# Lag blocks laid out by transfers through device memory, and the context's work moved between the latents' scan steps

## The chip, the cores and the metric

The kernel runs on one core of a Trainium2 chip. The time is that of one launch, in device microseconds. The kernel before took 1921.28 us (median of three runs, 1921.07 to 1925.02). The names of the engines are: PE for the matrix engine, DVE for the vector engine, ACT for the scalar engine, POOL for GpSimd, and SP for the engine that here only issues transfers (SPq is its queue).

## The reference, cut to what matters

One layer of a hybrid model is applied to 128 context tokens and to 512 latent tokens (width 1024). Everything is float32.

```
h   = rmsnorm(x) * (1 + sc1) + sh1            # sc, sh, g: from silu(cond) @ w_mod, 6 parts of 1024
z   = h @ w_in  ->  u (512), cb, cc, ch (512 each)
y1  = gelu(ssm(u) + d_skip * u);  y1 = y1 * sigmoid(y1 @ w_glu + b_glu)      # two complex scans
y2  = cb * conv3(cc * ch)                     # width 3, along the tokens
x   = x + g1 * (concat(rmsnorm(y1), rmsnorm_heads(y2)) @ w_out)
h   = rmsnorm(x) * (1 + sc2) + sh2
x   = x + g2 * peer(h)    # per head: scores, top 16 of 16 x 16 key pairs, gather 16 rows of expert_u and expert_v
y   = rmsnorm(x)
```

The scan starts from zero for the context and from given states for the latents. The last states of the context's scan are outputs too.

## The kernel before, in words

The kernel is written out by hand: each engine has one list of instructions in a fixed order, and semaphores join the lists. Nothing is planned by a scheduler, so the order of the code is the order on the engine, and an instruction that waits holds back everything behind it on its engine.

The scans are done in chunks of Q = 8 tokens: 16 chunks for the context, 64 for the latents. On PE, `chunk_sums` (sixteen groups g, of which the last eight belong to the backward scan) forms what each chunk adds to the state; ACT copies each group from PSUM into `HH` (semaphore `s_ev`). Inside a chunk the output comes from lag blocks: 64 matmuls on PE (`k_mm`) give one block for each lag and channel group, DVE adds them up in `Ksb` (`lag_blocks`, semaphore `k_ev`), and they must then be spread out so that the eight positions of a chunk stand in eight partition groups. That spread matrix is `M` (128 partitions, 32 groups, 128 columns, 2 MB). In the kernel before, PE spreads it by 2 x 32 matmuls with a selecting matrix (`esel`, line 662, `m_mm`), and ACT copies eight PSUM banks into `M` (line 1217, `m_ev`).

DVE then runs the scan over the chunks: sixteen steps for the context (lines 1571 to 1575, `scan_ctx` after the last), then fifteen steps that advance the four segments of the latents' scan at once, on tiles four times as wide, and then for each of the segments 2, 3 and 4 a correction (`segment_products`, `segment_add`, `segment_store`, lines 1598 to 1609). `scan_lat` says that `HH` is complete. ACT turns one half of it round into `Hb` (line 1244, `hb_ready`).

The context's own chain goes: context outputs of the scan (PE lines 697 to 702), gelu, turning, the gate's matmul (line 749), and beside it twelve convolution tiles (`conv_ctx`, line 675, each counts one on `zc_mm`; `zc_mm` 4, 8 and 12 end the three groups of four), the convolution itself on DVE, two norms (`head_sums`, `spread_heads`, `token_sums`, `spread_root`), and the output projection (`out_ctx`, line 788, `zoc_mm`). After it come the residual, the second norm (lines 1656 to 1668), the first query and scores (PE lines 826 and 833), the first top-k on DVE (lines 1679 to 1731), and with the indices the first gather on POOL (line 1935).

The latents' scan outputs are `y_lat`, eight pieces of 64 matmul records each (lines 766 to 771). They need `hb_ready`. In the kernel before two of the eight are put ahead of the first query, and six behind the scores. `spread_experts` (line 864), which hands the first indices to DVE and so to POOL, stands behind all of them.

All loads go through the one queue of SP, in the order of its list: the modulation weights (`load_mod`, 1 MB each, n = 0 to 23), the convolution tiles (`load_conv_ctx`, 0.5 MB each, six buffers), the gate's and the output's weights. A load waits on SP for its buffer: `load_mod(n)` until slab n-2 has been used on PE, the tiles 6 and up until four tiles earlier have been used, `woA` for slab 23 (`mod_mm` 24).

## Time and profile before

| | |
|---|---|
| Median of three runs | 1921.28 us |
| The profiled execution, its own time | 1922.27 us |
| Its span | 1920.1 us |
| PE busy | 62% |
| DVE busy | 72% |
| ACT, POOL busy | 19%, 38% |
| DMA's rate, mean | 392 GB/s |
| Chain that ended last | DMA 43%, PE 28%, DVE 23% |

The span is that of the instructions; about 2 us of the execution lie outside of it. The shares are means over stages of different kinds: the change touches only the stage from about 110 us to the first gather at 215.6 us. Rows are read as: start in us, duration in us, engine, line, operation, tiles; an "x" and a number at the end counts the records that were merged (a float32 matmul leaves two), and a bracket tells how long the engine was idle before and what ended that.

### The profile page before, as it was taken

To read this page: it belongs to the slowest core of one execution; us is meant where nothing else is said; L and a number is where in the kernel's file an instruction comes from. 1 tells how busy PE (TensorE), PEld (TensorE's weight loads), DVE (VectorE), ACT (ScalarE), POOL (GpSimd) and SP (SyncE) were. 2 spreads that over 40 slices of the span, in tenths; PEclk is the share of its full clock that TensorE was granted. 3 is DMA by queue.
4 is the path that set the end of the run, shared out by engine and by line. 5 is a ranking of instruction groups with operands and counts; after the bars stand their busy time and mean duration, and the time that the engine had idled before them with its cause. 6 is when DMAs were issued, how large, how long until landed. Compare 5 with 4: busy or idle time off the path is not lost.

```text
span 1920.1 us, 21154 instructions
## 1 busy us (share of the span) xinstructions
PE 1194.3 (62%) x7716; PEld 475.8 (25%) x7716; DVE 1382.6 (72%) x3664; ACT 373.5 (19%) x845; POOL 725.1 (38%) x666
## 2 busy tenths in 40 slices
PE   6989898999777777775543343544343454444434
PEld 3569644444322322221110000111000011111001
DVE  8968567777766766669777776677777678766664
ACT  5142441121122121111211110121111121111110
POOL 0000233344444434445434444444444354444440
PEclk9999999999878877775755555565555565555555
DMA  9855699999999999999999999999999999999994
GB/s 372 328 209 199 257 395 414 378 416 420 390 421 399 419 422 421 420 389 422 420 422 423 421 421 421 421 421 421 422 422 421 421 421 418 422 420 421 418 420 182
DMA packets 120968, 753.16 MB, mean 392 GB/s; under 512 B 12240, under 2 KB 27856, under 8 KB 33568
## 3 DMA queue, kind: packets, MB, share of 16 engines
q0 software_dynamic: 92160, 671.13, 84.5%
q1 hardware_dynamic: 28704, 80.69, 11.0%
q8 instruction: 60, 0.98, 0.2%
q14 instruction: 44, 0.36, 0.0%
HBM read 749.12 MB, written 11.04 MB: 396 GB/s over the span
## 4 chain that ended last, share of the span: by engine, by line
DMA 43%; PE 28%; DVE 23%; issue 2%; POOL 1%; ACT 1%; SPq 0%; DVEq 0%; POOLq 0%; ACTq 0%
DMA r<-table,gidx 31%; DVE r L1747 9%; DMA mix_r<-table,gidx 8%; PE bank L878 7%; PE bank L846 6%; PE bank L983 3%; DMA r<-w_mod 3%; DVE mix_r L1747 2%; PE bank L996 2%; PE bank L813 1%; POOL r L1935 1%; PE bank L962 1%; PE bank L855 1%; DVE i L1680 1%; PE bank L788 1%
## 5 line engine op out<-in xcount | busy, mean ns | idle before, releaser
L1935 POOL DMA_INDIRECT r<-table,gidx x542 | 607.7, 1121 | 865.3 <-PE bank L878 723.9
L1747 DVE CUSTOM_DVE_ANT_0 r<-r 128x1024 f32<-128x1024 f32 x542 | 658.1, 1220 | 246.5 <-DMA r<-table,gidx 246.0
L878 PE MATMUL bank<-r,cond 128*32 128x512 f32 x1432 | 327.2, 911 | 370.4 <-DVE cond L1759 295.2
L878 PE MATMUL bank<-r,wgt 128*32 128x512 f32 x736 | 166.8, 921 | 194.1 <-DVE wgt L1759 145.8
L1289 ACT ACTIVATE r<-r 128x2 f32<-128x2 f32 x320 | 65.1, 204 | 1013.1 <-DVE r L1747 1012.5
L878 PEld LDWEIGHTS bank<-r,cond 128*32 128x32 f32 x1432 | 37.1, 129 | 572.0 <-DVE cond L1759 437.2
L1935 POOL DMA_INDIRECT mix_r<-table,gidx x98 | 109.4, 1116 | 136.1 <-PE bank L878 117.0
L1747 DVE CUSTOM_DVE_ANT_0 mix_r<-mix_r,r 128x1024 f32<-128x1024 f32 x98 | 119.3, 1221 | 48.4 <-DMA mix_r<-table,gidx 48.2
L878 PE MATMUL bank<-mix_r,cond 128*32 128x512 f32 x264 | 91.1, 994 | 80.7 <-DVE cond L1759 63.4
L846 PE MATMUL bank<-hT_r,r 128*128 128x512 f32 x256 | 121.5, 630 | 0.9 <-ACT hT_r L1143 0.9
L878 PEld LDWEIGHTS bank<-r,wgt 128*32 128x32 f32 x736 | 18.9, 130 | 295.3 <-DVE wgt L1759 214.3
L1757 DVE SCALAR_TENSOR_TENSOR cond<-fold,r 128x32 f32<-128x32 f32 x168 | 34.8, 248 | 71.5 <-ACT r L1289 71.5
L846 PEld LDWEIGHTS bank<-hT_r,r 128*128 128x128 f32 x256 | 50.6, 203 | 75.8 <-issue 75.8
L1289 ACT ACT_TABLE_LOAD x51 | 65.4, 1283 | 0.9
L878 PE MATMUL bank<-mix_r,wgt 128*32 128x512 f32 x128 | 40.2, 930 | 38.2 <-DVE wgt L1759 35.6
L996 PE MATMUL bank<-mix_r,r 128*128 128x512 f32 x128 | 60.0, 611 | 0.0
L983 PE MATMUL bank<-hT_r,r 128*128 128x512 f32 x128 | 59.1, 604 | 0.0
L864 PEld LDWEIGHTS bank<-r,ident 128*32 128x32 f32 x1280 | 44.4, 140 | 43.6 <-DVE r L1719 36.8
L1747 DVE DVE_READ_ACCUMULATOR2_ANT r<- 128x1 f32 x640 | 52.6, 82 | 0.0
L1285 ACT ACT_TABLE_LOAD x40 | 51.3, 1283 | 0.7
L903 PE MATMUL bank<-mix_r,modrow 128*128 128x512 f32 x80 | 46.1, 712 | 3.2 <-ACT r L1304 1.9
L1757 DVE SCALAR_TENSOR_TENSOR wgt<-fold,r 128x32 f32<-128x32 f32 x88 | 18.3, 249 | 41.3 <-ACT r L1289 41.3
(367 smaller groups left out, 1637.1 us busy)
## 6 DMA issues: line engine op xcount, KB each, us to landing
r<-w_mod SPq DMA_DIRECT2D x24, 1024.0 KB, 9.7
r<-wq_heads SPq DMA_DIRECT2D x14, 1024.0 KB, 8.8
r<-table,gidx POOLq DMA_INDIRECT x542, 18.7
wq_heads<-w_query SPq DMA_DIRECT2D x8, 1024.0 KB, 12.1
r<-w_tiles SPq DMA_DIRECT2D x12, 512.0 KB, 7.8
x_r<-w_tiles SPq DMA_DIRECT2D x10, 512.0 KB, 6.0
hT_r<-xT SPq DMA_DIRECT2D x4, 640.0 KB, 6.1
r<-w_u SPq DMA_DIRECT2D x1, 2048.0 KB, 29.5
```

The costliest lines, as they stand in the source:

```text
L788: last = mm(bank[3 + m // 4][:, (m % 4) * P:(m % 4 + 1) * P], w[:, k, :], mixc[:, k, :], start=first and m in (0, 6) and k == ks[0], stop= ...
L846: last = mm(bank[2 + h][:, :], wqb[:, k, h * P:(h + 1) * P], hT[:, k, CTX:T], start=(k == 0), stop=(k == KD - 1))
L864: last = mm(bank[3][TG * s:TG * s + TG, 8 * tg:8 * tg + 8], ident[:, TG * tg:TG * tg + TG], gi[:, :, 4 * s:4 * s + 4], start=True, stop=True)
L878: last = mm(bank[ACC[b % 2][h]][to:to + TG, :], pair_weights(NPR * G + g)[:, e, :], rows[SLOT[G * TOPK + k]][:, D + h * 512:D + (h + 1) * ...
L903: last = mm(bank[at[h]][:, :], modrow[:, tg // 2, tg % 2 * P:(tg % 2 + 1) * P], h2tok[:, 512 * h:512 * h + 512], start=True, stop=True)
L983: last = mm(bank[(4, 5, 7)[r]][:, :], wtl[(tile + 2) % 3][:, k, :], hT[:, k, CTX:T], start=(k == 0), stop=(k == KD - 1))
L996: last = mm(bank[OUT_BANK[m % 3]][:, :], woA[:, m % 4, k, :], mixl[:, k, :], start=(k == 0), stop=(k == KD - 1))
L1285: A(e16, top, ACT.Exp, bias=small[:, 0:1], accum_out=small[:, 1:2]).then_inc(exp_done, 1)
L1289: A(gel[:, par, 2 * g:2 * g + 2], hid[:, par, 2 * g:2 * g + 2], ACT.Gelu_apprx_tanh).then_inc(gelu_done, 1)
L1747: V.tensor_tensor_reduce(row, row, h2r[tg], 1.0, 0.0, ALU.mult, ALU.add, hid[:, par, k:k + 1]).then_inc(dot_done, 1)
L1757: last = stt(pair_weights(n)[:, e, :], fold[:, :], gel[:, par, k:k + 1], gate[:, par, k:k + 1].broadcast_to([P, TG]), ALU.mult, ALU.mult)
L1935: G_.indirect_dma_start(rows[SLOT[j]], None, table, bass.IndirectOffsetOnAxis(gidx[:, e, k:k + 1], 0)).then_inc(row_in[SLOT[j]], 16)
```

## The change

The selecting matmuls and ACT's eight copies go. Instead SP writes `Ksb` to a tensor in device memory (`kfull`, 480 KB), waits for that, and reads it back by eight transfers into `M`. Each of them reads 512-byte pieces, 16 x 32 of them, and writes 16 partitions (256 KB). The context's outputs wait for these (`m_in`).

On PE the lag blocks' matmuls come ahead of groups 8 to 15 of the chunk sums; the first eight convolution tiles come ahead of the context's outputs, with the modulation slabs 20 and 21 between; slabs 22 and 23 come behind the outputs; the heads' norm comes ahead of the output projection, whose convolution half now is first; and all eight pieces of `y_lat` stand behind the first scores. On DVE `lag_blocks` comes first, four of the sixteen groups are copied by DVE in place of ACT (`s_back`), the two half-width products of a scan step become one of full width, the context's elementwise work is put between the fifteen latent steps, and the residual and the second norm come ahead of the segments 3 and 4. On SP the loads of the slabs 20 to 23 come behind the new transfers and behind the tiles 6 and 7.

```diff
@@ SP
-            for n in range(18, 24):
-                load_mod(n)
+            load_mod(18)
+            load_mod(19)
+            sp.wait_ge(k_ev, 1)
+            sp.dma_start(kfull.rearrange("(m p) x -> p m x", p=P), Ksb).then_inc(k_out, 16)
+            sp.wait_ge(s_mm, 8)
+            sp.wait_ge(k_out, 16)
+            lags = kfull.rearrange("(g i) x -> i g x", i=GC)
+            for i in range(Q):
+                sp.dma_start(M[GC * i:GC * i + GC, :, :], lags[:, :, (Q - 1 - i) * GC:(Q - 1 - i) * GC + P]).then_inc(m_in, 16)
             sp.wait_ge(zc_mm, 2)
             ...
             for q in range(6, 8):
                 load_conv_ctx(q)
-            sp.wait_ge(m_mm, 2)
+            for n in range(20, 24):
+                load_mod(n)
@@ PE
-            pe.wait_ge(k_ev, 1)
-            pe.wait_ge(s_ev, 16)
-            for a in range(2):
-                for s in range(Q):
             ...
-                mod_slab(20 + a)
-            mod_slab(22)
             ...
+            conv_ctx(0)
+            conv_ctx(1)
+            mod_slab(20)
+            mod_slab(21)
+            pe.wait_ge(m_in, 16 * Q)
+            pe.wait_ge(s_ev, 12)
+            pe.wait_ge(s_back, 4)
             ...
-            mod_slab(23)
-            conv_ctx(1)
+            conv_ctx(2)
             ...
             pe.wait_ge(ld_wo, 32)
-            out_ctx(True, range(KS), 1)
-            out_ctx(False, range(KS, KD), 2)
+            out_ctx(True, range(KS, KD), 1)
+            out_ctx(False, range(KS), 2)
             ...
-            y_lat(0, 2)
-            y_lat(0, 3)
-            for i in range(4):
-                y_lat(1, i)
+            pe.wait_ge(hb_ready, 1)
+            pe.wait_ge(mod_free, 6)
+            for n in range(2):
+                for i in range(4):
+                    y_lat(n, i)
@@ DVE
-                link(tt(ta, prev, re, ALU.mult),
-                     tt(tb[:, :, 0, :], prev[:, :, 1, :], im[:, :, 0, :], ALU.mult),
-                     tt(tb[:, :, 1, :], prev[:, :, 0, :], im[:, :, 1, :], ALU.mult))
+                link(tt(ta, prev, re, ALU.mult), tt(tb, prev[:, :, ::-1, :], im, ALU.mult))
             ...
+            advance_rest(1, 7)
             ...
+            advance_rest(7, 10)
+            dve.wait_ge(zc_mm, 12)
             ...
+            advance_rest(10, 12)
```

The order on SP's queue before, from the modulation slabs on. `w_mod` are the slabs (x6 counts 18 to 23), `w_tiles` with a wait on `zc_mm` are first the gate's two tiles, then the convolution tiles:

```order
L411 DMA r<-w_mod 128x2048 [waits mod_mm] x6
L447 DMA r<-w_tiles 128x1024 [waits zc_mm]
L447 DMA r<-w_tiles 128x1024
L416 DMA x_r<-w_tiles 128x1024 [waits zc_mm] x2
L451 DMA mix_r<-w_query 128x8x256 [waits m_mm]
```

And in the changed kernel:

```order
L412 DMA r<-w_mod 128x2048 [waits mod_mm] x2
L447 DMA kfull<-mix_r 128x4x240 [waits k_ev]
L452 DMA r<-kfull 16x32x128 [waits k_out,s_mm]
L452 DMA r<-kfull 16x32x128 x7
L455 DMA r<-w_tiles 128x1024 [waits zc_mm]
L455 DMA r<-w_tiles 128x1024
L417 DMA x_r<-w_tiles 128x1024 [waits zc_mm] x2
L412 DMA r<-w_mod 128x2048 [waits mod_mm] x4
L460 DMA mix_r<-w_query 128x8x256
```

The write and the eight reads now stand ahead of the gate's tiles, of the tiles 6 and 7, and of four of the six slabs.

On PE, the changed kernel between the sixth convolution tile and the gelu of the context's outputs (L673 is a convolution tile, L537 a modulation slab, L695 to L700 the outputs, L709 their turning):

```order
L673 MATMUL bank<-hT_r,x_r 128x128 [waits wtc_in0]
...
L673 MATMUL bank<-hT_r,x_r 128x128 [waits wtc_in1]
...
L537 MATMUL bank<-r,cond 32x256 [waits wm_in0]
...
L537 MATMUL bank<-r,cond 32x256 [waits wm_in1]
...
L695 MATMUL bank<-r 32x128 [waits k_ev,s_back,hbc_ready,s_ev,m_in]
...
L697 MATMUL bank<-r 16x128 x8
...
L537 MATMUL bank<-r,cond 32x256 [waits wm_in0]
...
L709 MATMUL bank<-ident,r 128x128 [waits yc_gelu]
```

Before, the same outputs came ahead of every convolution tile:

```order
L662 MATMUL bank<-mix_r,wgt 32x512 [waits s_ev,k_ev]
...
L528 MATMUL bank<-r,cond 32x256 [waits wm_in0]
...
L662 MATMUL bank<-mix_r,wgt 32x512 [waits m_ev] x2
...
L697 MATMUL bank<-r 32x128 [waits hbc_ready,m_ev]
...
L675 MATMUL bank<-hT_r,r 128x128 [waits wtc_in4,m_ev]
```

So the tiles' and the slabs' loads are now waited for ahead of the outputs.

On DVE, the changed kernel from the residual's second half to the first top-k (L1598 to L1609 are a segment's correction, L1663 and L1670 to L1674 the second norm, L1679 raises `scan_lat`, L1689 is the top-k):

```order
L1656 SCALAR_TENSOR_TENSOR x_r<-bank,modT,x_r 128x128 [waits zoc_mm]
...
L1599 TENSOR_TENSOR r<-r 128x1024
L1663 RECIPROCAL frs<-frs 128x1 [waits rms_c,dve_seq]
...
L1603 TENSOR_TENSOR r<-r 128x1024
...
L1670 TENSOR_TENSOR hT_r<-x_r,bank 128x4x128 [waits x1c_ready,inv_mm,dve_seq]
...
L1674 TENSOR_SCALAR hT_r<-hT_r,gs,modT 128x128 [waits mod_ready,dve_seq]
...
L1598 TENSOR_TENSOR r<-r 128x1024
...
L1679 COPY small<-eps_c 128x1 [waits dve_seq]
...
L1689 MAX r<-r 128x8 [waits sc_ev]
```

Before, all segments and `scan_lat` (L1650) came ahead of the residual:

```order
L1603 TENSOR_TENSOR r<-r 128x1024 [waits dve_seq]
...
L1650 COPY small<-eps_c 128x1 [waits dve_seq]
L1656 SCALAR_TENSOR_TENSOR x_r<-bank,modT,x_r 128x128 [waits zoc_mm,ld_xc]
...
L1659 RECIPROCAL frs<-frs 128x1 [waits rms_c]
...
L1664 TENSOR_TENSOR hT_r<-x_r,bank 128x4x128 [waits x1c_ready,inv_mm]
...
L1679 MAX r<-r 128x8 [waits sc_ev]
```

Two of the three later segments are behind the residual now, and with them `scan_lat`.

## Rows read from the trace of the kernel before

**Rows 1.** Windows: busy PE, PEld, DVE, ACT, POOL; granted clock, DMA share, GB/s

```profile
215.00:505.00 290.00, 269.75 (x1381) 130.19 (x1381) 198.79 (x541) 75.39 (x142) 109.34 (x98) 0.98 0.99 403
...
900.00:1400.00 500.00, 229.17 (x1304) 54.61 (x1304) 370.19 (x969) 78.64 (x183) 217.59 (x199) 0.55 1.01 421
```

**Rows 2.** Timeline, all engines, from the end of the segments to the first gather

```profile
188.14 0.15 DVE L1650 COPY small<-eps_c 128x1 f32<-128x1 f32 x1
188.33 1.91 ACT L1244 ACTIVATE r<-r 128x2048 f32<-128x2048 f32 x1 [9.03 <-DVE small L1650]
...
203.72 0.66 PE L766 MATMUL bank<-r 128*64 128x128 f32 x8
204.31 0.49 DVE L1679 MAX8 r<-r 128x8 f32<-128x128 f32 x2 [4.48 <-ACT r L1270]
...
213.99 0.88 PE L864 MATMUL bank<-r,ident 128*32 128x8 f32 x32
...
215.11 0.17 DVE L1731 CAST gidx<-bank 128x16 uint32<-128x16 f32 x1
...
215.58 1.12 POOL L1935 DMA_INDIRECT r<-table,gidx  x1 [48.58 <-DVE gidx L1731]
```

**Rows 3.** Timeline of PE and DVE: lag blocks, context's outputs, first convolution tiles

```profile
109.66 1.07 PE L528 MATMUL bank<-r,cond 128*32 128x256 f32 x16
...
116.66 1.82 PE L645 MATMUL bank<-r 128*32 128x128 f32 x57
120.09 2.06 PE L645 MATMUL bank<-r 128*32 128x128 f32 x68 [1.60 <-issue]
...
122.38 0.69 DVE L1557 COPY mix_r<-bank 128x512 f32<-128x512 f32 x1 [1.43 <-PE bank L645]
...
137.58 0.65 PE L697 MATMUL bank<-r 128*32 128x128 f32 x16 [1.57 <-ACT r L1219]
...
144.87 3.84 PE L675 MATMUL bank<-hT_r,r 128*128 128x128 f32 x32
```

**Rows 4.** Timeline of DVE: first products of successive scan steps, context, then latents

```profile
118.04 0.22 DVE L1571 TENSOR_TENSOR mix_r<-r,AR 128x64 f32<-128x64 f32 x1
...
119.02 0.23 DVE L1571 TENSOR_TENSOR mix_r<-r,AR 128x64 f32<-128x64 f32 x1
...
136.69 0.42 DVE L1571 TENSOR_TENSOR r<-r,AR 128x256 f32<-128x256 f32 x1
...
138.47 0.43 DVE L1571 TENSOR_TENSOR r<-r,AR 128x256 f32<-128x256 f32 x1
```

**Rows 5.** Issues of transfers: count, KB of each, median us to landing

```profile
x_r<-xT SPq DMA_DIRECT2D x1, 512.0 KB, 4.4
```

**Rows 6.** The two gate tiles (0.5 MB each) on an idle queue, line 447

```profile
L447 SPq DMA_DIRECT2D r<-w_tiles x2: 328/380/433, 148.7 to 149.1; - x2
...
DMA to landing us min/median/max: 3.7/4.2/4.6
```

**Rows 7.** Timeline of PE and DVE from the convolution to the second norm

```profile
164.13 1.11 DVE L1619 TENSOR_SCALAR mix_r<-mix_r,colv 128x128 f32<-128x128 f32 x4
...
173.11 1.95 PE L675 MATMUL bank<-hT_r,x_r 128*128 128x128 f32 x16
...
183.09 1.22 DVE L1598 TENSOR_TENSOR r<-r 128x1024 f32<-128x1024 f32 x1
185.51 3.74 PE L788 MATMUL bank<-mix_r,r 128*128 128x128 f32 x32
...
192.86 1.13 DVE L1656 SCALAR_TENSOR_TENSOR x_r<-bank,modT,x_r 128x128 f32<-128x128 f32 x4 [2.38 <-PE bank L788]
...
197.37 0.69 DVE L1664 TENSOR_TENSOR hT_r<-x_r,bank 128x512 f32<-128x512 f32 x1 [0.51 <-PE bank L731]
```

**Rows 8.** Timeline of PE: the same sixteen matmuls after a wait, and next

```profile
537.49 8.91 PE L846 MATMUL bank<-hT_r,r 128*128 128x512 f32 x16 [0.94 <-ACT hT_r L1143]
...
547.32 7.13 PE L846 MATMUL bank<-hT_r,r 128*128 128x512 f32 x16
```

More of the change, by code:

```diff
@@ L621, in _, with chunk_sums @@
             mod_slab(16)
-            pe.wait_ge(bpt_ev, 17)
-            for g in range(16):
-                if g >= 2:
-                    pe.wait_ge(s_ev, g - 1)
+            def chunk_sums(g):
+                if g >= 10 and g % 2:
+                    pe.wait_ge(s_back, (g - 9) // 2)
+                elif g >= 2:
+                    pe.wait_ge(s_ev, min(g - 1, 4 + g // 2))
                 for j in range(2):
@@ L633, in _ @@
                 last.then_inc(s_mm, 1)
-                if g == 7:
-                    mod_slab(17)
+            pe.wait_ge(bpt_ev, 17)
+            for g in range(8):
+                chunk_sums(g)
+            mod_slab(17)
             pe.wait_ge(bd_ready, 1)
@@ L647, in _ @@
                 last.then_inc(k_mm, 1)
+            for g in range(8, 16):
+                chunk_sums(g)
             mod_slab(18)
             mod_slab(19)
[L652 to L666 removed]
             def conv_ctx(r):
[L670 removed]
                 for i in range(4):
@@ L751, in _ @@
             mod_turn(2)
-            conv_ctx(2)
+            head_sums()
+            spread_heads()
             def y_lat(n, i, terms=range(5)):
@@ L779, in out_ctx @@
                 for m in (0, 1, 2, 3, 6, 7, 4, 5) if first else range(KD):
-                    if first and m == 2:
-                        head_sums()
                     if first and m == 6:
-                        spread_heads()
+                        pe.wait_ge(sqc_ready, 2)
+                        token_sums(256, sqx[0], True, True)
+                    if first and m == 4:
+                        spread_root(0)
                     if m == 4:
@@ L1201, in _ @@
             act.wait_ge(bp_ready, 2)
-            for g in range(16):
+            for g in (*range(8), *range(8, 16, 2)):
                 d, pr = g // 8, (g % 8) * 2
@@ L1212, in _ @@
                 last.then_inc(s_ev, 1)
-            for n in range(8):
-                a, j = n // 4, n % 4
-                act.wait_ge(m_mm, a + 1)
-                A(M[:, 2 * j + a::8, :], bank[MBANK[a][j]][:, :].rearrange("p (q x) -> p q x", q=4), ACT.Copy).then_inc(m_ev, 1)
+            act.wait_ge(zc_mm, 4)
+            A(ccx.rearrange("p k t -> p (k t)"), bank[0][:, :], ACT.Copy).then_inc(ccx_ev, 1)
             act.wait_ge(scan_ctx, 1)
@@ L1373, in _ @@
             take_scores(0)
+            act.wait_ge(scan_lat, 1)
+            A(Hb, HH[:, NCH - 1:NCC - 1:-1, :, 1, :], ACT.Copy).then_inc(hb_ready, 1)
             exps(0)
@@ L1578, in spread @@
                 return v[:, :, :].rearrange("p (a r) x -> p a r x", a=1).broadcast_to([P, n, 2, NQ])
-            dve.wait_ge(s_ev, 16)
+            lag_blocks()
+            for g in range(9, 16, 2):
+                pr = g % 8 * 2
+                dve.wait_ge(s_mm, g + 1)
+                for r in range(2):
+                    src = bank[4 + g % 2][:, 0:4 * NCH].rearrange("p (q r c) -> p c r q", q=2, r=2)[:, :, r, :]
+                    V.tensor_copy(HH[:, NCC:0:-1, r, 1, pr:pr + 2], src[:, 0:NCC, :])
+                    last = V.tensor_copy(HH[:, NCH - 1:NCC:-1, r, 1, pr:pr + 2], src[:, NCC + 1:NCH, :])
+                last.then_inc(s_back, 1)
+            dve.wait_ge(s_back, 4)
+            dve.wait_ge(s_ev, 12)
             link(V.tensor_copy(fin[:, :, :], HHs[:, NCC, :, :]))
@@ L1590, in _, with advance_rest @@
             rest = slice(1, NJ)
-            for i in range(1, SEG):
-                link(advance(seg[:, rest, i - 1, :, :], seg[:, rest, i, :, :], many_a, many_b, spread(AR, NJ - 1), spread(AI, NJ - 1)))
+            def advance_rest(lo, hi):
+                for i in range(lo, hi):
+                    link(advance(seg[:, rest, i - 1, :, :], seg[:, rest, i, :, :], many_a, many_b, spread(AR, NJ - 1), spread(AI, NJ - 1)))
             def segment_products(j):
@@ L1669, in _ @@
             last.then_inc(xsc_ready, 1)
+            segment_products(4)
+            segment_add(4)
+            segment_store(4)
+            V.tensor_copy(small[:, 2:3], eps_c[:, :]).then_inc(scan_lat, 1)
             NT = 23
```

105 lines of the change are left out of this document (40 added, 65 removed).

## Prediction

> **What bounds the kernel now.** I read the windows first, to see which stage the change can touch. After the first gather the DMA engines are busy all the time, at 403 GB/s to 505 us and at 421 GB/s from 900 to 1400 us [rows 1]: the gathers are one stream that runs at the rate of the memory until the end. Whatever comes before the first gather is a lead-in. If the first gather starts later by some us, the end does too, since nothing behind it has slack to give back. So the whole question is when the cast of the first indices (line 1731) ends: at 215.11 + 0.17 = 215.3 us in the kernel before, and POOL follows 0.3 us later [rows 2].
>
> Next the timeline around it. DVE ends its top-k before PE lets it go on: PE starts `spread_experts` (line 864) at 213.99, right behind the last of six `y_lat` pieces, which began at 203.72 [rows 2]. That is 10.27 / 6 = 1.71 us a piece. So the first gather hangs on the end of `y_lat`, and DVE's own work only through the start of the top-k at 204.31.
>
> **The rule for break-even.** In the changed kernel all eight pieces stand behind the scores and wait for `Hb`. They take 8 x 1.71 = 13.7 us, and `Hb` takes 0.2 + 1.9 us after `scan_lat` (188.14 to 190.24) [rows 2]. To be as early as before, `y_lat` must start at 214.0 - 13.7 = 200.3, so `scan_lat` must be there at about 198.2 us. It was at 188.1 before, with nothing but DVE's own work ahead of it. The change puts in front of it the residual, the second norm and the wait for the output projection.
>
> **Part 1, up to the end of the context's scan.** The lag matmuls took from 116.66 to 122.2, with a gap of 1.6 us in them [rows 3]. Moved ahead of eight chunk sums, they start when slab 17 ends, at 109.66 + 1.07 = 110.7 [rows 3], and end at 116.3. `lag_blocks` takes 1.7 us on DVE, which is idle then: `k_ev` at 118.0. The eight chunk sums follow in the 6.0 us that they took before (110.7 to 116.66): 122.3. Four copies on DVE instead of ACT hide beside them, the last adds 0.6, the start of the scan 0.5: 123.4 instead of 118.04. A context step takes 119.02 - 118.04 = 0.98 us [rows 4]. Two products of 32 columns become one of 64. I take 0.92, because the second start (0.10 us) goes and the longer product costs about 0.04; the bounds are 0.88 and 1.0. Sixteen steps are 14.7: `scan_ctx` at 138.1 instead of 136.7, although 3.1 us of `lag_blocks` and its wait have left the scan. A latent step takes 1.78 [rows 4] and by the same reckoning 1.72 after, so 0.9 us over fifteen.
>
> **Part 2, the transfers.** This is where the price is. A 0.5 MB load on an idle queue lands after 3.7 us, and the one behind it 1.3 us later [rows 6] (148.7 + 3.7 and 149.1 + 4.6). So a load costs 1.3 us of the queue per 0.5 MB and 2.4 us once (1.4 ahead, 1.0 behind). 1 MB costs 2.6. The write of `kfull` (480 KB) then costs about 1.6 + 2.4: issued at 118.0, in at 122.0. The reads may only then be issued, and their data start at 123.4.
>
> How long is a read of 256 KB into 16 partitions? The trace has none. The lower bound: a 0.5 MB load in pieces of 512 bytes over 128 partitions took 4.4 us [rows 5], so 2.0 on the queue, and half the bytes take 1.0 us. The upper bound: 1 MB over 128 partitions puts 8 KB in each in 2.6 us; if what a partition takes in is the limit, 16 KB a partition need 5.2 us. I take the middle by ratio, 2.3 us each and 18.4 for the eight, since the narrow target must cost something and neither row is near to it. All end at 141.8.
>
> The Trainium skill, page "SBUF — State Buffer", section "Door 1: The DMA port swizzle", says that DMA bandwidth depends on how many of sixteen ports the partitions reach, and gives 104 GB/s for the partitions 0 to 15, against 328 for all. An estimate from that is 2.5 us a transfer, and the end would be 1.6 us later than by my 2.3. The same page, section "Can I just issue two DMAs to hit both halves?", says that two such transfers to different partitions serialize, so the eight would not overlap either. No row here shows a narrow transfer.
>
> Behind them on the queue stand: the gate's two tiles (2.6), tile 6 (1.3, lands at 146.7), tile 7 (148.0), slab 20 (150.6), slab 21 (153.2). PE meanwhile: slabs 18 and 19 to 124.3, six convolution tiles of 1.84 each (a quarter of the 7.3 us that four take: 3.84 and its like [rows 3]) to 135.3. Then it waits 11 us for tile 6. Two tiles and the slab 20 are done by about 153, and slab 21 waits for its load: 154.2. A cost that this hides: after a wait of this kind PE's clock is at 1.2 instead of 2.4 GHz for a while. Sixteen matmul records that began after PE had been waiting took 8.91 us, the same sixteen next 7.13 [rows 8], and the granted clock is a mean of 0.98 to 505 us and 0.55 from 900 us, where PE waits for most of the time [rows 1]. So 1.8 us more for the tiles 6 and 7, which fits in ahead of slab 21.
>
> The context's outputs take 137.58 to 144.87 = 7.3 us [rows 3]: 161.5. Slabs 22 and 23: 163.5. Only then SP issues `woA` (2 MB, 5.2 at the same rate), which stands ahead of the tiles 10 and 11: 163.5 + 1.4 + 5.2 + 1.3 + 1.0 gives tile 10 at 172.4, and two tiles end `zc_mm` 12 at about 176.0. Before it was at 173.11 + 1.95 = 175.06 [rows 7]. DVE has done six latent steps, the convolution and three more steps by 161.5 and waits 14 us. (The convolution is three groups of four instructions of 128 columns, 1.1 each [rows 7], and one product: 4.2.)
>
> **Part 3, from `zc_mm` 12 to the first gather.** PE: gate 3.7 (sixteen matmuls, as the 3.74 at 185.51 [rows 7]), `mod_turn` 1.2, `head_sums` 0.9: 181.8. Root and reciprocal 0.5, `spread_heads` 1.0, and the scaling by DVE (1.1), with one latent step and the hand-overs between: 185.0. Output projection: convolution half 7.4 (two of the 3.74 [rows 7]) and 1.1 for sums and root, then the other half 7.4: 201.0. This second half was in the kernel before the work of 185.5 to 192.7, so PE is 8.3 us later here. Residual 1.1, then DVE puts segment 3 (products 2.4, the rest 2.6) ahead of the norm's scaling: 207.3 against 197.37 [rows 7]. Scaling 2.4 and segment 4, as 183.09 to 188.14 = 5.0 [rows 2, 7]: `scan_lat` at 214.8. `Hb` 2.1, `y_lat` 13.7, `spread_experts` 0.9, cast 0.3: 231.8.
>
> **Sum.** 231.8 - 215.3 = 16.5 us later. The profiled execution took 1922.27 us, 1.0 above the median of the runs, so 1938.8 for it and 1937.8 by the median. What is removed (the selecting matmuls on PE and ACT's eight copies) is in these times already: PE has no shortage of time in part 2, it waits.
>
> **Rivals.**
> 1. The narrow transfers run like wide ones, 1.0 us each. Then all in part 2 moves up by 10.4 us: `zc_mm` 12 at 165.6, indices at 221.4, so 6.1 later: 1927.4. Even with free reads PE's own work sets part 2 and the indices come at about 219.4: 1925.4. For it: packets of 512 bytes cost little more than large ones. Against it: the target has an eighth of the partitions. At 5.2 us each it is 23 us worse than my sum, 1961.
> 2. Faster: DVE without waits. Work from 123.4 to the end of segment 4 is 14.7 + 25.8 (latent steps) + 4.2 (convolution) + 15.0 (segments) + 8.6 (residual, norms, products) = 68.3, so `scan_lat` at 191.7 and the indices at 208.7, 6.6 us earlier: 1914.7. It decides from the 6.4 us of waiting that DVE can afford before 198.2. For it: DVE waits for most of the time from 188.3 to 204.3 [rows 2], and the new order puts segments there. Against it: in part 3 alone DVE waits some 7 us, for head sums, roots and the projection, and 14 at tile 11.
> 3. The delay is absorbed: 1919 to 1924. The stage to 505 us has PE busy 93% [rows 1], not DMA alone, so a shifted start could meet fewer collisions. Against it: that work too is queued behind the first indices.
>
> **Numbers.** Forecast (late by narrow transfers, 1933 to 1944) 0.58; rival 1 at 1.0 to 1.4 us a transfer 0.22; the dear end, over 1944, 0.06; absorbed 0.08; faster 0.06. Small and large misses in the chain are some us each way. The range that leaves out no more than 2 in 10 is 1925 to 1944. A measurement tells apart 0.2%, 3.8 us, so slower is over 1925.1: 0.58 + 0.06 + most of 0.22, 0.84; same 0.10; faster 0.06.
>
> **What would show it.** The rows of the eight reads: median to landing, and when the last is in (141.8 + 1.0 by me, 132 by rival 1). PE's wait ahead of the seventh convolution tile, for a load, about 11 us. DVE's wait for the twelfth tile, 14 us. `y_lat` in one piece of 13.7 us, ahead of line 864's successor, starting at 216.9. If `scan_lat` comes before 198 us, the forecast is wrong at its root; if the cast is at 231.8 and the end is not 16 us later, the stream of gathers was not the bound that I read.

## The result and the profile after

The changed kernel takes 1955.03 us (median of 6 runs, 1952.33 to 1956.74), the kernel before 1923.45 in the same runs (1921.07 to 1927.53). The ratio is 1.0158 with a 95% interval of 1.0148 to 1.0168, so the change costs 30.4 us, 28.5 to 32.3. Forecast were 16.5 us, and the range ended at 1944. The profiled span is 1954.9 us against 1920.1.

The timeline after, PE, DVE and POOL (start us, duration, engine, line, operation; in brackets the idle time before it and what ended it):

```profile
147.33 6.57 PE L673 MATMUL bank<-hT_r,x_r 128*128 128x128 f32 x32 [11.94 <-DMA x_r<-w_tiles]
...
153.83 1.93 PE L537 MATMUL bank<-r,cond 128*32 128x256 f32 x32
155.58 0.62 PE L695 MATMUL bank<-r 128*32 128x128 f32 x16
...
160.60 0.42 PE L695 MATMUL bank<-r 128*32 128x128 f32 x8
164.62 0.66 PE L695 MATMUL bank<-r 128*32 128x128 f32 x8 [3.59 <-issue]
...
180.07 5.47 PE L673 MATMUL bank<-hT_r,x_r 128*128 128x128 f32 x32 [4.97 <-DMA x_r<-w_tiles]
...
185.64 0.69 DVE L1623 TENSOR_TENSOR mix_r<-mix_r,bank 128x512 f32<-128x512 f32 x1 [22.28 <-PE bank L673]
...
194.69 6.76 PE L788 MATMUL bank<-mix_r,r 128*128 128x128 f32 x32 [1.61 <-DVE mix_r L1631]
...
220.91 5.65 PE L821 MATMUL bank<-hT_r,mix_r 128*128 128x128 f32 x32 [3.45 <-ACT hT_r L1139]
...
230.01 0.66 PE L765 MATMUL bank<-r 128*64 128x128 f32 x8 [2.27 <-ACT r L1365]
...
245.13 0.88 PE L859 MATMUL bank<-r,ident 128*32 128x8 f32 x32
...
246.72 1.13 POOL L1945 DMA_INDIRECT r<-table,gidx  x1 [55.69 <-DVE gidx L1741]
```

The large waits lie where the forecast put them. PE stands 11.9 us for the seventh convolution tile (line 673), and 5.0 us for tile 10; the outputs (line 695) start at 155.6; DVE waits 22.3 us for the last tile (line 1623). All eight pieces of `y_lat` run as one block from 230.01 to 245.13, and the first gather comes at 246.72 instead of 215.58 [rows 2]: 31.1 us later, and the span is 34.8 us longer. The block of work is the same; it is later, and slower. Two tiles that took 3.84 us [rows 3] take 6.57 here, the first projection group 6.76 instead of 3.74 [rows 7], and inside the outputs PE waits 3.59 us for nothing that the profile shows.

The page's issues and the windows of the transfers (windows: length; busy us of PE, PEld, DVE, ACT, POOL; granted clock; DMA share; GB/s):

```profile
r<-kfull SPq DMA_DIRECT2D x8, 256.0 KB, 12.6
...
kfull<-mix_r SPq DMA_DIRECT2D x1, 480.0 KB, 4.1
```

```profile
122.00:128.00 6.00, 6.00 (x80) 4.98 (x79) 4.79 (x26) 0.29 (x3) 0.00 (x0) 1.00 1.19 121
128.00:134.00 6.00, 6.00 (x57) 6.00 (x55) 5.31 (x27) 0.60 (x1) 0.00 (x0) 1.00 1.29 106
134.00:140.00 6.00, 1.39 (x13) 1.20 (x11) 5.45 (x24) 1.47 (x2) 0.00 (x0) 0.95 1.24 107
140.00:146.00 6.00, 0.00 (x0) 0.00 (x0) 5.66 (x15) 0.44 (x1) 0.00 (x0) 0.50 1.08 290
```

From 128 to 140 us, with the reads at the head of the queue, the DMA engines move 106 and 107 GB/s. 256 KB at that rate are 2.5 us a read, where I had taken 2.3, and in the trace the eight reads land from 126.12 to 143.65 us, 2.50 us apart in the mean. The Trainium skill's page "SBUF — State Buffer", section "Door 1: The DMA port swizzle", gives 104 GB/s, measured at 1 MiB, for partitions 0 to 15. This trace agrees, and for eight groups of 16 partitions.

One window answers where the 31 us went: from 110 us to the start of the first `spread_experts` (line 864 before, 859 after), before and after:

```profile
110.00:213.99 103.99, 97.83 (x1597) 82.81 (x1589) 77.13 (x258) 30.28 (x79) 0.61 (x1) 1.00 0.51 185
```

```profile
110.00:245.13 135.13, 101.17 (x1457) 89.89 (x1445) 76.87 (x240) 24.41 (x54) 0.61 (x1) 0.85 0.56 159
```

PE was idle for 104.0 - 97.8 = 6.2 us and is now idle for 135.1 - 101.2 = 34.0, so 27.8 more. It is busy 3.3 us longer although the 64 selecting matmuls (8.7 us; an f32 matmul is two records in the trace, so 128 of them) are gone: the rest of the work takes 12.1 us more at a mean clock of 0.85. 27.8 + 12.1 - 8.7 is 31.1, up to rounding. DVE's work adds nothing to it; DVE is busy for 77 us in both.

### The profile page after: what moved, and what is told of

Its sections match the earlier page's. It is cut to its first block, busy times and chain, and to the rows that moved or that the text cites. A ratio compares the mean times of both kernels' runs of the same rounds, so it can differ in the third digit from the quotient of the medians.

```text
span 1954.9 us, 20863 instructions
## 1 busy us (share of the span) xinstructions
PE 1202.6 (62%) x7588; PEld 483.3 (25%) x7588; DVE 1383.0 (71%) x3646; ACT 368.0 (19%) x822; POOL 729.7 (37%) x666
## 3 DMA queue, kind: packets, MB, share of 16 engines
q1 hardware_dynamic: 33456, 83.28, 12.1%
## 4 chain that ended last, share of the span: by engine, by line
DMA 38%; PE 32%; DVE 24%; issue 3%; ACT 2%; POOL 1%; DVEq 0%; SPq 0%; POOLq 0%; ACTq 0%
DMA r<-table,gidx 28%; DVE r L1757 9%; DMA mix_r<-table,gidx 8%; PE bank L873 7%; PE bank L841 6%; PE bank L978 3%; PE bank L991 2%; DVE mix_r L1757 2%; PE bank L808 1%; POOL r L1945 1%; PE bank L585 1%; DMA x_r<-w_tiles 1%; PE bank L673 1%; PE bank L537 1%; PE bank L898 1%
## 5 line engine op out<-in xcount | busy, mean ns | idle before, releaser
L873 PE MATMUL bank<-mix_r,wgt 128*32 128x512 f32 x128 | 40.3, 945 | 35.0 <-DVE wgt L1769 32.3
L898 PE MATMUL bank<-mix_r,modrow 128*128 128x512 f32 x80 | 50.3, 769 | 3.2 <-ACT r L1294 1.9
L859 PE MATMUL bank<-r,ident 128*32 128x8 f32 x1280 | 47.1, 196 | 1.4 <-DVE r L1729 1.4
## 6 DMA issues: line engine op xcount, KB each, us to landing
wq_heads<-w_query SPq DMA_DIRECT2D x8, 1024.0 KB, 11.1
```

The source lines that it names most:

```text
L859: last = mm(bank[3][TG * s:TG * s + TG, 8 * tg:8 * tg + 8], ident[:, TG * tg:TG * tg + TG], gi[:, :, 4 * s:4 * s + 4], start=True, stop=True)
L873: last = mm(bank[ACC[b % 2][h]][to:to + TG, :], pair_weights(NPR * G + g)[:, e, :], rows[SLOT[G * TOPK + k]][:, D + h * 512:D + (h + 1) * ...
L898: last = mm(bank[at[h]][:, :], modrow[:, tg // 2, tg % 2 * P:(tg % 2 + 1) * P], h2tok[:, 512 * h:512 * h + 512], start=True, stop=True)
```

## The experiments

Ratios are against the kernel before, run on the same chip each time. The first gather's start is from the profiled execution; it was 215.58 before and 246.72 after.

| run | us | ratio (95%) | first gather |
|---|---|---|---|
| e1 after, M spread on PE | 1949.3 | 1.0139 (1.0122 to 1.0156) | 240.01 |
| e2 after, wide reads | 1946.0 | 1.0118 (1.0101 to 1.0136) | 237.60 |
| e3 after, half the bytes | 1944.3 | 1.0113 (1.0096 to 1.0131) | 235.28 |
| e4 before, with the transfers | 1945.6 | 1.0116 (1.0099 to 1.0134) | 237.03 |
| e5 e1, tiles ahead of woA | 1941.7 | 1.0098 (1.0073 to 1.0123) | 236.22 |
| e6 after, tiles ahead of woA | 1945.7 | 1.0121 (1.0098 to 1.0144) | 241.67 |
| e7 e1, tail of before | 1952.2 | 1.0156 (1.0134 to 1.0178) | 243.60 |
| e8 e5, tail of before | 1945.5 | 1.0121 (1.0098 to 1.0145) | 239.33 |
| e9 after, PE kept busy (too long) | 1968.0 | 1.0230 (1.0212 to 1.0248) | 259.05 |
| e10 e5, no loads beside outputs | 1947.8 | 1.0123 (1.0106 to 1.0140) | 238.35 |
| e11 e6, transfers on ACT's queue | 1950.3 | 1.0136 (1.0119 to 1.0153) | 242.85 |
| e12 before, merged products | 1921.2 | 0.9986 (0.9977 to 0.9996) | 213.34 |
| e13 after, PE kept busy | 1947.4 | 1.0128 (1.0109 to 1.0146) | 239.11 |
| e14 e5, last tiles ahead of outputs | 1939.3 | 1.0089 (1.0069 to 1.0108) | 227.64 |
| e15 e14, first query's load later | 1940.2 | 1.0085 (1.0063 to 1.0108) | 231.78 |

**e1: the order without the transfers.**

```diff
@@ SP
-            sp.dma_start(kfull.rearrange("(m p) x -> p m x", p=P), Ksb).then_inc(k_out, 16)
             ...
@@ PE
+            spread_lags(0)          # the selecting matmuls, 32 each
             ...
             conv_ctx(0)
             ...
+            spread_lags(1)
             conv_ctx(1)
-            pe.wait_ge(m_in, 16 * Q)
+            pe.wait_ge(m_ev, 8)     # ACT's eight copies into M
```

> The changed kernel, but the lag blocks are spread as in the kernel before: 64 selecting matmuls in two lots (ahead of the convolution's tiles 0 to 3 and of 4 to 7) and eight copies on ACT; no transfer through device memory. Everything else keeps the new order. Theory A (the eight narrow reads hold everything behind them on SP's queue, and the order itself is harmless): tile 6 is there when PE wants it, DVE's wait of 22.3 us ahead of the context's last convolution product falls under 4 us, the first gather comes at 216 to 222 us instead of 246.7, and the time is 1920 to 1930 us. Theory B (the new order costs by itself: latents' outputs in one piece behind the last scan step, convolution and norms ahead of the scan): the first gather stays later than 228 us and the time over 1933 us.

Tile 6 was on time, but theory A fell: 27 of the 30 us stay, and the gather and the time are where theory B had them. Which part of the order costs, this run does not tell; e5 to e8 ask that. DVE waited nearly as long as in the changed kernel (timeline of PE and DVE):

```profile
171.97 6.22 PE L666 MATMUL bank<-hT_r,x_r 128*128 128x128 f32 x32 [5.92 <-DMA x_r<-w_tiles]
...
178.31 0.69 DVE L1639 TENSOR_TENSOR mix_r<-mix_r,bank 128x512 f32<-128x512 f32 x1 [20.39 <-PE bank L666]
```

**e2, e3: the price of a read.**

```diff
# e2
-                sp.dma_start(M[GC * i:GC * i + GC, :, :], lags[:, :, (Q - 1 - i) * GC:(Q - 1 - i) * GC + P]).then_inc(m_in, 16)
+                sp.dma_start(M[:, 4 * i:4 * i + 4, :], lags[:, :, (Q - 1 - i) * GC:(Q - 1 - i) * GC + P]).then_inc(m_in, 16)
# e3
-                sp.dma_start(M[GC * i:GC * i + GC, :, :], lags[:, :, ...])
+                sp.dma_start(M[GC * i:GC * i + GC, 0:16, :], lags[:, 0:16, ...])
```

> The changed kernel with eight reads of the same 256 KB in pieces of the same 512 bytes, but each into all 128 partitions instead of 16 (M then holds the lag blocks in the wrong places; this part of the computation is left wrong). Theory A (the price is that of 16 partitions): the reads take 0.7 to 1.0 us each instead of 2.3 to 2.6, the last lands by 131 us instead of 144, tile 6 starts before 138 us instead of 147.3, and the time is 1918 to 1930 us. Rival (the price is that of 512-byte pieces, or of a read behind a write): nothing moves, 1952 to 1957 us.

> The changed kernel with eight reads of half the bytes each (128 KB, groups 0 to 15; groups 16 to 31 of M are left as they were, so that part of the computation is left out). Theory A (a read costs by its bytes into 16 partitions): each takes 1.2 us instead of 2.4, tile 6 starts near 138 us instead of 147.3, and the time falls by 8 to 14 us, to 1941 to 1947. Rival (a price per transfer, whatever its bytes): tile 6 moves by less than 3 us, time 1950 to 1956 us.

Windows of e2, then the row of tile 6 in the timeline of PE, of e2 and of e3:

```profile
122.00:128.00 6.00, 6.00 (x80) 4.98 (x79) 4.82 (x26) 0.27 (x3) 0.00 (x0) 1.00 1.04 271
128.00:134.00 6.00, 6.00 (x57) 6.00 (x56) 5.31 (x27) 0.60 (x1) 0.00 (x0) 1.00 1.03 303
```

```profile
136.21 3.84 PE L673 MATMUL bank<-hT_r,x_r 128*128 128x128 f32 x32 [0.84 <-DMA x_r<-w_tiles]
```

```profile
136.37 3.84 PE L673 MATMUL bank<-hT_r,x_r 128*128 128x128 f32 x32 [1.49 <-DMA x_r<-w_tiles]
```

The same bytes in the same pieces move at 271 to 303 GB/s into 128 partitions (the second window holds other loads too), so 0.9 us a read. Tile 6 came 11.1 us earlier with wide reads, and 11.0 with half the bytes, so the reads do cost what I said, and e3 falls into theory A's range. But e2 misses it by 16 us: the times fell by only 7.7 us (1.0158 to 1.0118) and 8.7, the first gather by 9.1 and 11.4. The other 22 to 23 us have another cause.

**e4: the transfers in the old order.**

```diff
@@ SP
             load_mod(19)
+            sp.dma_start(kfull.rearrange("(m p) x -> p m x", p=P), Ksb).then_inc(k_out, 16)
             ...
@@ PE
-            for a in range(2):      # the selecting matmuls
             ...
+            pe.wait_ge(m_in, 16 * Q)
```

> The kernel before with the transfers alone: the lag blocks go through device memory with the same write and eight reads, while DVE, the convolution, norms and the latents' outputs keep the old order (lag blocks inside the context's scan, k_ev at about 122 us; the context's outputs ahead of the convolution). Theory A: the write starts at about 125 us and the reads end at about 150; the outputs start at 150 to 153 instead of 137.6 us, the convolution's tiles 0 to 5 lie behind them, and the time is 1933 to 1948 us. Theory B (the transfers are mostly hidden and the new order costs): 1920 to 1928 us.

Windows of e4, then its timeline of PE:

```profile
122.00:128.00 6.00, 0.33 (x7) 0.00 (x0) 5.38 (x32) 0.00 (x0) 0.00 (x0) 0.90 0.50 125
128.00:134.00 6.00, 0.00 (x0) 0.00 (x0) 5.38 (x31) 0.00 (x0) 0.00 (x0) 0.50 1.27 101
...
140.00:146.00 6.00, 0.00 (x0) 0.00 (x0) 5.66 (x17) 0.00 (x0) 0.00 (x0) 0.50 1.28 106
```

```profile
150.46 1.93 PE L536 MATMUL bank<-r,cond 128*32 128x256 f32 x16 [28.14 <-DMA r<-w_mod]
...
157.42 1.93 PE L536 MATMUL bank<-r,cond 128*32 128x256 f32 x16 [2.18 <-DMA r<-w_mod]
159.13 1.08 PE L694 MATMUL bank<-r 128*32 128x128 f32 x16
```

Here the queue alone does it: slab 20 stands behind the reads, PE is idle for 28.1 us, and the outputs start at 159.1 (forecast 150 to 153: the slabs 20 to 22, which stand behind the reads, I had left out; the time is in theory A's range). So either half of the change costs 22 to 27 us by itself, and both together 30. That the two do not add fits DVE's waits: it stands still for convolution tiles at much the same time in all three kernels, 20.4 us in e1 (to 178.3) and 22.3 with both (to 185.6), for the twelfth tile, and 22.0 in e4 (161.7 to 183.7), for the eighth. In the kernel before it has no such wait.

**e5 to e8: what the order's delay hangs on.** In e5 and e6 SP's order, in e7 and e8 DVE's and PE's tail:

```diff
# e5 on e1, e6 on after
-            for q in range(8, 10):
+            for q in range(8, 12):
                 load_conv_ctx(q)
             sp.wait_ge(mod_mm, 24)
             sp.dma_start(woA, w_o[:, 0:4, :, :]).then_inc(ld_wo, 16)
-            for q in range(10, 12):
-                load_conv_ctx(q)
# e7 on e1, e8 on e5: DVE, then PE
+            segment_products(3)
             ...
+            V.tensor_copy(small[:, 2:3], eps_c[:, :]).then_inc(scan_lat, 1)
             residual_ctx(0)
@@
+            y_lat(0, 0)
             ...
             spread_root(1)
+            y_lat(0, 1, range(1, 5))
```

> The kernel of the first experiment (new order, lag blocks spread by PE and ACT) with one more edit: SP issues the convolution's tiles 10 and 11 ahead of woA (2 MB) instead of behind it. In the first experiment PE waited 5.9 us for tile 10 and then ran two tiles at the low clock, so that DVE stood still for 20.4 us. Theory C (the new order makes DVE's whole queue wait for the last convolution tile, and each us of that wait comes out at the end one for one): the wait falls by 8 us, the time is 1938 to 1944 us against 1949. Theory D (the delay is that of the tail, latents' outputs in one piece behind a scan that ends behind the residual): less than 3 us, over 1946.

> The changed kernel with the tiles 10 and 11 issued ahead of woA, nothing else. Theory C: PE's wait of 5.0 us for tile 10 and the 1.7 us of low clock behind it go, the time falls by 5 to 8 us, to 1947 to 1950 us. Theory D: no more than 2 us, 1953 to 1957.

> The kernel of the first experiment with the tail of the kernel before: DVE does the latents' segments 3 and 4 ahead of the context's residual and norm, and PE does two of the eight pieces of the latents' outputs ahead of the first query. Theory C: DVE is 27 us late already by its waits, so this moves work about: the time falls by 1 to 5 us, to 1944 to 1948. Theory D (the tail is the cost): it falls by more than 15 us, to under 1934.

> The first experiment's kernel with both edits, the tiles 10 and 11 ahead of woA and the tail of the kernel before. Theory C: the two gains add, 1935 to 1942 us. Theory D: as the tail alone gives, under 1934. Either way it is the new order's head (convolution ahead of the outputs and norms among the scan's steps) that is left in it.

Tiles that no longer stand behind a 2 MB load gave 7.9 us (1.0139 to 1.0098) and 7.1 (1.0158 to 1.0121), as theory C said. In the profiled execution of e5 PE no longer waits for tile 10 (5.9 us in e1), but DVE's wait fell by 2.4 us only, to 18.0, and not by the 8 expected: it was the slowest of the four (1944.7 us), and the gaps in its outputs were 6.6 us against 3.0 in e1 (below). The old tail gave nothing: e7 and e8 are 3.3 and 4.4 us slower than e1 and e5, with intervals that overlap. Theory D is dead, and theory C, which had both faster, missed these two. With the segments and `scan_lat` ahead of the residual PE stood 9.8 us for the residual's squares (timeline of PE, e7):

```profile
216.55 1.86 PE L727 MATMUL bank<-ones,mix_r 128*128 128x1 f32 x8 [9.81 <-ACT mix_r L1267]
```

The two halves of the tail, DVE's and PE's, were not tried one by one.

**e9, e13: the clock.** Matmuls that nothing uses stand where PE would wait; e13 has half of them.

```diff
+            def keep_warm(b, n):
+                for _ in range(n):
+                    mm(bank[b][:, :], ident[:, :], hT[:, 0, CTX:T], start=True, stop=True)
@@ conv_ctx
+                    if q == 6:
                         ...
+                        keep_warm(3, 13)      # e9: 25
+                    if q == 10:
                         ...
+                        keep_warm(0, 5)       # e9: 10
@@ ahead of the projection, the query and y_lat
+            keep_warm(3, 1)                   # then 3 and 2; e9: 4, 7 and 4
```

> The changed kernel with matmuls added that compute nothing used, where PE stands still: 25 of 128x512 ahead of the convolution's tile 6 (11.1 us at full clock, in a wait of 11.9), 10 ahead of tile 10 (4.4 in 5.0), 4 ahead of the output projection, 7 ahead of the first query (3.1 in 3.5), 4 ahead of the latents' outputs. Theory E (PE's low clock after each wait costs 11 us of the 31: PE is busy for 101.2 us from 110 us to the first spread of the expert indices, where the same work without the spread took some 90 before): the granted clock is 0.97 or more in this stretch, the tiles 6 and 7 take 3.8 us instead of 6.6, the first half of the projection 3.9 instead of 6.8, the query 3.9 instead of 5.7, and the time falls by 5 to 10 us, to 1945 to 1950 us. Rival (the low clock lies beside other waits): less than 2 us, 1953 to 1957 us.

> The changed kernel with matmuls of 128x512 added that compute nothing used (0.87 us each, as e9 showed): 13 ahead of the convolution's tile 6 (11.3 us in a wait of 11.9), 5 ahead of tile 10 (4.3 in 5.0), 1 ahead of the output projection, 3 ahead of the first query (2.6 in 3.5), 2 ahead of the latents' outputs (1.7 in 2.3). Theory E (PE's low clock behind its waits is 11 us of its busy time, and more than half of that on the path): the time falls by 5 to 10 us against the changed kernel's 1955, to 1945 to 1950 us. Rival: the low clock lies beside other waits, less than 2 us, 1953 to 1957.

One such matmul takes 0.87 us, not the 0.44 I had planned with (I had read a record for a matmul), so in e9 they outlasted every wait and cost 14 us. In e13 they fit (timeline of PE, then a window as above):

```profile
149.34 3.84 PE L685 MATMUL bank<-hT_r,x_r 128*128 128x128 f32 x32 [2.47 <-DMA x_r<-w_tiles]
...
192.51 3.81 PE L800 MATMUL bank<-mix_r,r 128*128 128x128 f32 x32 [0.55 <-DVE mix_r L1646]
```

```profile
110.00:237.53 127.53, 112.79 (x1513) 89.25 (x1505) 76.83 (x240) 24.70 (x55) 0.61 (x1) 0.97 0.62 170
```

The clock is 0.97 instead of 0.85, and the 24 added matmuls are 23.3 of the 112.8 us busy (three of them ran partly at the low clock), so the kernel's own work takes 89.5 us instead of 101.2. In the kernel before it is 97.8 - 8.7 = 89.1, so nearly all that the work grew by is the clock's. The first gather is 7.6 us earlier (0.9 of them from a shorter gap in the outputs), the time 5.8 us less (1.0158 to 1.0128). Theory E holds, at the low side of its range. The Trainium skill, page "TensorE: Matmul & The Clock Gate", section "What's actually happening", puts the penalty of the ramp, the work done before the clock is up, at under 1% of a typical kernel's span. This case agrees: what e13 took off is 0.3% of the span, though it is a fifth of what the change costs.

**e10, e15: the gaps in the outputs.** The outputs are 160 small matmuls (320 records) in 7 us.

```diff
# e10 on e5
+            sp.wait_ge(yc_mm, 2)
             for n in range(22, 24):
                 load_mod(n)
# e15 on e14
+            sp.wait_ge(yc_mm, 2)
             sp.dma_start(wqa, w_query[:, :, 0:DQ]).then_inc(ld_first, 16)
```

> The kernel with the lag blocks spread by PE and the tiles 10 and 11 ahead of woA, with one wait more on SP: the slabs 22 and 23, and so all loads behind them, are issued only when the context's outputs are done, so that no load runs beside the outputs. Theory F (the gaps of 2.5 and 4.1 us in the 320 small matmuls of the outputs, in which PE waits for nothing that the profile shows, come from its instructions arriving late behind the loads; in the kernel before, with the DMA engines 5% busy there, the gap was 0.3 us): the gaps fall under 0.7 us in all and the outputs take 7.0 to 8.0 us instead of 13.6; PE then waits 3 to 6 us for slab 22, and the time is 1938 to 1944 us. Rival (the gaps belong to the place in the program, whatever the DMA engines do): they stay over 3 us, and the time is 1943 to 1950.

> As e14, but the first query's weights (1 MB) are loaded only behind the context's outputs, so that, where the slabs 22 and 23 have landed by then, nothing loads beside the outputs. Theory F (PE's gaps in the outputs come from its instructions arriving late behind loads): the gaps in the outputs fall under 1.5 us in all, and the time is 2 to 5 us under that of e14. Rival: no difference over 1 us.

The timeline of PE and the window of the outputs, of e5, then of e10:

```profile
154.06 0.32 PE L710 MATMUL bank<-r 64*16 64x128 f32 x5 [2.45 <-issue]
...
161.08 0.80 PE L705 MATMUL bank<-r 128*32 128x128 f32 x9 [4.13 <-issue]
```

```profile
148.78:163.68 14.90, 8.32 (x325) 5.70 (x317) 8.09 (x24) 0.00 (x0) 0.00 (x0) 0.86 0.96 350
```

```profile
155.32 0.49 PE L708 MATMUL bank<-r 128*32 128x128 f32 x9 [1.12 <-issue]
...
161.83 1.93 PE L531 MATMUL bank<-r,cond 128*32 128x256 f32 x16 [4.94 <-DMA r<-w_mod]
```

```profile
148.61:156.89 8.28, 7.16 (x324) 5.10 (x316) 7.90 (x24) 0.01 (x1) 0.00 (x0) 1.00 0.02 7
```

With the DMA engines 96% busy the gaps are 6.6 us and the outputs take 14.9; with 2% they are 1.1 us, and 8.3. So the loads beside them make the gaps, as theory F said, apart from a rest of 1.1 (I had said under 0.7). What PE waits for can be read from the traces too. They have packets of 16 KB and of the kind `instruction`, on a queue of their own (section 3 of the changed kernel's page: packets, MB, share of the 16 engines):

```profile
q8 instruction: 59, 0.97, 0.2%
```

From 100 to 260 us of the 17 traces there are 52 gaps of more than 0.3 us in which PE waits for no semaphore, and each ends 1.2 to 1.6 us after one of these packets has landed. In the 39 gaps of up to 2 us the packet had started 0.7 to 2.2 us before PE stopped; in the 13 longer ones it started only after PE had stopped. In e5 the gaps begin at 151.62 and 156.95, the packets run from 151.79 to 152.72 and from 158.78 to 159.76, and PE goes on at 154.06 and 161.08. In e10 the packet of the gap that is left started at 152.93, and PE stopped at 154.20. So it is code that PE waits for, and beside loads the code's packet starts late. That this queue is PE's own is inferred from these times. The kernel before fits: its 26% (the expectation has 5%) are loads that land by 139.9 us, and its gap of 0.3 comes at 142.6.

The gain is lost at once. PE then waits 4.9 us for slab 22, and e10 at 1.0123 is no faster than e5 at 1.0098; its time is in the rival's range. In e15 the gaps are 0.8 us against 2.0 in e14, and the time is the same (1.0085 and 1.0089): theory F is right about the gaps and the rival about the time.

**e11: another queue.**

```diff
-            sp.dma_start(kfull.rearrange("(m p) x -> p m x", p=P), Ksb).then_inc(k_out, 16)
+            act.dma_start(kfull.rearrange("(m p) x -> p m x", p=P), Ksb).then_inc(k_out, 16)
             ...     # and the eight reads
```

> The changed kernel with the tiles 10 and 11 ahead of woA, and the write and the eight reads of the lag blocks issued by ACT on its own queue instead of SP's. Theory A (tile 6 waits because it stands behind the reads on one queue): tile 6 starts at 135 to 140 us instead of 148.7, the reads end at 144 to 150, and the time falls by 3 to 9 us against the same kernel on SP's queue (1945.7), to 1937 to 1943. Rival (the reads fill the DMA engines that every load needs, whatever the queue): tile 6 starts after 145 us, 1944 to 1948.

The timeline of PE:

```profile
145.62 5.41 PE L665 MATMUL bank<-hT_r,x_r 128*128 128x128 f32 x32 [10.78 <-DMA x_r<-w_tiles]
...
155.70 1.91 PE L529 MATMUL bank<-r,cond 128*32 128x256 f32 x16 [3.67 <-DMA r<-w_mod]
158.77 1.08 PE L687 MATMUL bank<-r 128*32 128x128 f32 x16 [1.15 <-DMA r<-kfull]
```

SP issued tile 6 at 129.5 us, where it was 134.6 in e6, and still it landed only at 145.6, 3.1 us earlier than in e6, and PE waited 10.8 us for it. The rival holds for tile 6, and the time is even above its range (1.0136 against e6's 1.0121, with intervals that overlap): the narrow reads fill the engines that every load needs, and standing behind them on one queue is at most 3 us of the wait. The loads on the other queue did pass reads: the last three of the eight landed at 150.7, 156.8 and 158.7, behind tile 6, and the outputs waited for the last (158.77). The comparison is not quite clean, since ACT issued the write 3.2 us later than SP in e6, behind its own copies.

**e12: one part alone, on the kernel before.**

```diff
-                     tt(tb[:, :, 0, :], ...), tt(tb[:, :, 1, :], ...))
+                link(tt(ta, prev, re, ALU.mult), tt(tb, prev[:, :, ::-1, :], im, ALU.mult))
```

> The kernel before with one part of the change alone: on DVE the two products of a scan step that cross the real and imaginary halves are one instruction, 32 instructions less in the scan and three less in the segments. DVE's work to the last scan step is some 2.5 us shorter. Theory G (PE is the bound of this stretch: it is idle for 6.2 of 104 us): within 1.5 us of the kernel before. Rival (DVE's scan is the bound): 2 to 3 us faster.

The timeline of PE at the start of the outputs:

```profile
135.47 0.64 PE L697 MATMUL bank<-r 128*32 128x128 f32 x16 [0.90 <-ACT r L1219]
```

The time is in the rival's range: 2.7 us faster (0.8 to 4.4, which does not exclude theory G's 1.5). The outputs start at 135.47 instead of 137.58 [rows 3], behind the context's scan (0.8 of these 2.1 us is a shorter gap in the lag matmuls, which the edit does not touch). PE waits there in both kernels for ACT's copy of what the scan gives, 1.57 us before and 0.90 here. So up to there DVE is on the path of the kernel before, which I had read as PE's. This kernel is the only one that beats both.

**e14: DVE's wait taken away by order.**

```diff
             mod_slab(21)
+            pe.wait_ge(m_ev, 5)
+            conv_ctx(2)                 # loads: ahead of slabs 22 and 23
             ...                         # the context's outputs
+            head_sums()                 # ACT: its square ahead of the gelu
             mod_slab(22)
             ...
-            conv_ctx(2)
```

> The kernel e5 (lag blocks spread by PE and ACT, tiles 10 and 11 early) with the context's last four convolution tiles ahead of its outputs on PE (their loads ahead of the slabs 22 and 23), the head sums behind the outputs, and ACT's square for them ahead of the first gelu. Theory C (what is left in e5 is DVE standing still for 18 us for the last tile, since the scan's steps stand behind it): that wait falls under 3 us, a shorter one for the heads' root takes its place, the first gather comes at 222 to 230 us instead of 236.2, and the time is 1927 to 1936 us. Rival (the chain from the gate's product through the norms and the projection sets the end, and it hangs on the outputs): the gather moves by less than 3 us, 1939 to 1943.

The timeline of DVE and PE:

```profile
168.20 0.20 DVE L1643 RECIPROCAL frs<-frs 128x8 f32<-128x8 f32 x1 [6.82 <-ACT frs L1238]
...
202.30 5.15 PE L834 MATMUL bank<-hT_r,mix_r 128*128 128x128 f32 x32 [3.14 <-ACT hT_r L1152]
...
210.91 0.66 PE L778 MATMUL bank<-r 128*64 128x128 f32 x8 [2.27 <-ACT r L1382]
```

DVE's wait for the tile is gone, one of 6.8 us for the heads' root has come, and the gather is 8.6 us earlier, inside the range given. But the time is 3 us over its own range and inside the rival's, and 1.7 us under e5's by ratio, with intervals that overlap. The 8.6 us compare the slowest of e5's executions with the fastest of e14's four (1935.4). So the traces show that DVE's wait can be taken away by order; that this makes the kernel faster is not shown. What is left in e14 is a tail of short waits of PE (3.1, 2.3, 2.0, 1.1 us and less); other work was not tried in them.

## Why the prediction was wrong

Right were the bound (the first gather), the place and order of the large waits, and the price of a read: 2.5 us against 2.3. DVE's wait for the twelfth tile came where it was forecast, but took 22.3 us and not 14. Step by step, forecast against measured:

| | forecast | measured | difference |
|---|---|---|---|
| `scan_ctx` | 138.1 | 138.5 | 0.4 |
| tile 6 | 146.7 | 147.3 | 0.6 |
| outputs start | 154.2 | 155.6 | 1.4 |
| outputs end | 161.5 | 167.1 | 5.6 |
| `woA` issued | 163.5 | 170.6 | 7.1 |
| `zc_mm` 12 | 176.0 | 185.5 | 9.5 |
| `y_lat` starts | 216.9 | 230.0 | 13.1 |
| cast ends | 231.8 | 246.4 | 14.6 |

**The first failed step: "the context's outputs take 137.58 to 144.87 = 7.3 us".** I carried a duration over to a place with other traffic. They took 11.5 us, 4.2 more: 3.6 of gap, of the kind that e10 shows to come from the loads beside them, and the rest by the low clock behind the gap. The DMA engines were 26% busy in that stretch before, and 98% after (windows, before and after):

```profile
137.58:144.87 7.29, 6.99 (x320) 5.13 (x320) 6.88 (x21) 1.16 (x1) 0.00 (x0) 1.00 0.26 105
155.58:167.10 11.52, 7.93 (x328) 5.69 (x321) 7.41 (x22) 0.00 (x0) 0.00 (x0) 0.84 0.98 353
```

**The second: "So 1.8 us more for the tiles 6 and 7, which fits in ahead of slab 21."** I charged the clock once. In the trace it was at 0.50 six times between 139 and 235 us, each time behind waits or gaps, short ones too: it cost 2.7 us in the tiles 6 and 7, 1.5 in the slabs 22 and 23, 1.7 in the tiles 10 and 11, 3.0 in the projection, 1.8 in the query, 1.4 in `y_lat`. The last five are 9.4 us; with the 4.2 of the outputs and the 1.4 by which they started late that is 15.0, against the 14.6 of the table. In e13, where the clock stays up, the gather is 7.6 us earlier. The row that I quoted for it (8.91 against 7.13 us [rows 8]) was too mild: a group behind a wait took up to 1.8 times its length here (6.76 us for 3.74).

**The third is in a rival.** "Even with free reads ... the indices come at about 219.4: 1925.4." e1, with no reads, had its gather at 240.0, and e2, with reads at 0.9 us, 1946 us instead of 1927. There I was wrong by 19 us, more than in the forecast itself. I had worked out the order's own cost as a by-product of the reads' and never by itself: it has the same gap in the outputs, the same clock, and the same 2 MB load ahead of tile 10. By e1 and e4 each of the two costs 22 to 27 us alone, so a range that begins at 1925 left out what the order costs.

Rival 2 (faster) fell on DVE: from the start of the scan to the end of segment 4 it worked 64 us (reckoned: 68.3), but it also waited 39, 22 of them in one place. Rival 3 (absorbed) fell too: the span's delay is 1.0 to 1.2 times that of the first gather in most runs, 34.8 for 31.1 here. What the extra 1 to 5 us are was not looked into.

## What to carry to other kernels

When an engine has no idle time in a stretch, an order is worth what it does to that engine's waits: 9 us of its work taken off gave nothing, since 28 us of waiting came in and the rest of its work grew by 12. Price each part of a compound change alone, as if the rest were not made; two parts that each cost 25 us can cost 30 together, and then undoing one of them helps little. And a duration read in a quiet stretch at full clock holds only in such a stretch: behind waits of some us expect the low clock, and where hundreds of small instructions run beside loads, take a gap.
